# A hybrid mLSTM, window attention and expert layer on one core: narrow loads, gate columns, output-gate weights and row maxima rearranged in the input and mLSTM stages

## The reference, cut to what matters

```python
h = _rmsnorm(x, norm_mix); z = h @ w_in
gates = mif + b_if
ig, logf = gates[..., :4], log_sigmoid(gates[..., 4:])
# _mlstm, one step per chunk of 128 tokens, four heads of width 256
bcum = cumsum(fc)
dlog = where(causal, bcum[:, None] - bcum[None, :] + ic[None, :], -inf)
mt = maximum(bcum + m, max(dlog, -1))             # the row maximum
dmat = exp(dlog - mt[:, None]); sc = exp(bcum + m - mt)
s = (q @ k.T) * dmat
num = s @ v + sc * (q @ c);  den = sum(s) + sc * (q @ n)
hout = num / maximum(abs(den), exp(-mt))
c_new = wc * c + kw.T @ v;   n_new = wc * n + sum(kw)
```

## Time and profile before

| what | value |
|---|---|
| times of three runs | 2022.81, 2023.15 (median), 2028.75 us |
| the profiled execution | 2026.17 us, its span 2024.5 us, mean granted TensorE clock 0.943 |
| busy: PE, PEld, DVE, ACT, POOL | 88%, 83%, 42%, 34%, 17% of the span |
| the four heads, by PE's time line | about 51 to 628 us |
| DMA | 280.67 MB, 139 GB/s over the span |

### The profile page before, as it was taken

How to read it: one execution, slowest core, us unless ns; L and a number is a source line. 1 busy time by engine, 2 the same in 40 slices (tenths; PEclk the granted TensorE clock), 3 DMA queues, 4 the chain that set the end, 5 groups by cost and what they waited for, 6 DMA issues and landing times.

```text
span 2024.5 us, 33235 instructions
## 1 busy us (share of the span) xinstructions
PE 1787.5 (88%) x12631; PEld 1682.0 (83%) x12632; DVE 857.2 (42%) x1589; ACT 697.3 (34%) x1221; POOL 344.1 (17%) x275
## 2 busy tenths in 40 slices
PE   5989998998999999999999958989899469999960
PEld 4978997988989999899999948979899369998850
DVE  5423123122122110444444444233522659998856
ACT  4323122222222221332233333121202348888742
POOL 3001001001001000000000022000002037776634
PEclk9989999999999999999999978989999779999985
DMA  5033205105115222232222134332413369999967
GB/s 173 1 105 106 92 22 164 54 8 169 42 34 176 88 81 88 73 109 68 68 68 69 55 144 149 123 100 86 161 54 133 124 224 371 380 373 367 364 222 261
DMA packets 142962, 280.67 MB, mean 139 GB/s; under 512 B 35844, under 2 KB 106252, under 8 KB 130540
## 3 DMA queue, kind: packets, MB, share of 16 engines
q1 hardware_dynamic: 104608, 210.57, 30.3%
q0 software_dynamic: 18768, 48.79, 6.7%
q10 hardware_dynamic: 19488, 19.87, 2.8%
HBM read 227.36 MB, written 69.70 MB: 147 GB/s over the span
## 4 chain that ended last, share of the span: by engine, by line
PE 78%; DMA 8%; DVE 5%; issue 4%; ACT 2%; SPq 1%; POOL 1%; DVEq 0%; POOLq 0%; ACTq 0%; PEldq 0%
PE pb L770 18%; PE pb L771 17%; PE pb L772 17%; DMA stg<-in_w_gate_e 5%; PE pw L1057 3%; PE pq L1077 3%; PE pb L1065 2%; PE pw L770 2%; PE pw L771 2%; PE pw L772 2%; PE pw L861 1%; PE pq L844 1%; ACT aTh L1274 1%; PE pq L770 1%; PE pq L854 1%
## 5 line engine op out<-in xcount | busy, mean ns | idle before, releaser
L770 PE MATMUL pb<-aTh,wlo 128*128 128x352 f32 x1152 | 388.0, 337 | 29.3 <-issue 16.0
L770 PE MATMUL pb<-whi,aTl 128*128 128x256 f32 (+1 forms) x1296 | 377.3, 291 | 8.5 <-DVE aTl L2053 3.8
L771 PE MATMUL pb<-aTl,whi 128*128 128x352 f32 x1152 | 379.0, 329 | 0.0
L772 PE MATMUL pb<-aTh,whi 128*128 128x352 f32 x1152 | 378.9, 329 | 0.0
L771 PE MATMUL pb<-wlo,aTh 128*128 128x256 f32 (+1 forms) x1296 | 367.6, 284 | 0.0
L772 PE MATMUL pb<-whi,aTh 128*128 128x256 f32 (+1 forms) x1296 | 365.5, 282 | 0.0
L770 PEld LDWEIGHTS pb<-aTh,wlo 128*128 128x128 f32 x1152 | 225.0, 195 | 33.8 <-issue 27.1
L770 PEld LDWEIGHTS pb<-whi,aTl 128*128 128x128 f32 (+1 forms) x1296 | 234.8, 181 | 21.6 <-issue 11.8
L1644 DVE TENSOR_TENSOR wlo<-stage,whi 128x2048 fp32r<-128x2048 f32 x74 | 169.2, 2288 | 182.8 <-ACT whi L1274 182.8
L772 PEld LDWEIGHTS pb<-whi,aTh 128*128 128x128 f32 (+1 forms) x1296 | 235.7, 182 | 0.9
L771 PEld LDWEIGHTS pb<-wlo,aTh 128*128 128x128 f32 (+1 forms) x1296 | 234.4, 181 | 2.1
(11 more groups left out here) (396 smaller groups left out, 3020.4 us busy)
## 6 DMA issues: line engine op xcount, KB each, us to landing
stg<-in_w_down_e SPq DMA_DIRECT2D x32, 1024.0 KB, 14.1
stage<-in_w_in SPq DMA_DIRECT2D x30, 1024.0 KB, 5.3
stage<-in_w_gate_e SPq DMA_DIRECT2D x16, 1024.0 KB, 13.8
stage<-in_w_up_e SPq DMA_DIRECT2D x16, 1024.0 KB, 14.8
stg<-in_w_gate_e SPq DMA_DIRECT2D x16, 1024.0 KB, 14.7
stg<-in_w_up_e SPq DMA_DIRECT2D x16, 1024.0 KB, 15.0
zt_scratch<-zo ACTq DMA_DIRECT2D x80, 128.0 KB, 1.7
zg_scratch<-go ACTq DMA_DIRECT2D x48, 176.0 KB, 1.8
```

Source lines behind the costliest of these rows:

```text
L770: pe.matmul(out, ll, rh, start=first, stop=False)
L771: pe.matmul(out, lh, rl, start=False, stop=False)
L772: return pe.matmul(out, lh, rh, start=False, stop=last)
```

## The change

1. **Input loads.** `cst` is issued ahead of `gB`. The second, third and fourth x tiles follow the first without a narrow load between; `wif` is loaded after the fourth, `bif` after the last. The splits of `wif` move from step 2 to step 5 (ACT) and from step 4 to step 7 (DVE).
2. **Gate columns.** PE transposes them between feature groups 10 and 11 of the first head, not after group 11: four tiles into each of the two banks, the ninth and the state rows into `pw`, without waiting for a copy. DVE copies four tiles at once.
3. **Loads of a head.** `weights(3)` is issued before the wait for the gate columns and the state loads.
4. **Row maxima.** `nmrow` is split once into three bf16 terms, at partitions 0, 32 and 64 of `nmt`. Each head copies a selecting column (ones in the head's three rows) into `hrow`; the product in `s1` and in `head_sets` is now `hrow` by `nmt` in bf16 with K=68. The multiplication into `nmh` is gone.

```diff
@@ -34,2 +34,3 @@
 MH, MD = 4, 256
+NM = 64 + MH
 AH, AG, AD = 16, 4, 64
@@ -140,3 +141,4 @@
             msampb = a1("msampb", [TS, TS], BF16)
-            ones4 = a1("ones4", [MH, 128])
+            hsel = a1("hsel", [NM, MH])
+            hrow = a1("hrow", [NM, 128], BF16)
             gcol = a1("gcol", [128, NT, 128])
@@ -144,4 +146,3 @@
             wcb = a1("wcb", [128, 2 * NB])
-            nmrow = a1("nmrow", [MH, T + 2 * NB])
-            nmh = a1("nmh", [MH, T + 2 * NB])
+            nmt = a1("nmt", [NM, T + 2 * NB], BF16)
             Ce = a1("Ce", [128, 2, MD + 1])
@@ -170,2 +171,4 @@
             with sg:
+                nmrow = alloc(sg, "nmrow", [MH, T + 2 * NB])
+                nmb = alloc(sg, "nmb", [MH, T + 2 * NB], BF16)
                 gi = alloc(sg, "gi", [MH, T])
@@ -578,5 +583,5 @@
                 if t == 0:
-                    sp.dma_start(gB[:, :], norm_mix.to_broadcast([128, D])).then_inc(ld_c, 16)
                     sp.dma_start(cst[:, :], cst_d).then_inc(ld_c, 16)
-                if t == 1:
+                    sp.dma_start(gB[:, :], norm_mix.to_broadcast([128, D])).then_inc(ld_c, 16)
+                if t == NX - 1:
                     sp.wait_ge(init_v, 1)
@@ -585,5 +590,5 @@
                         sp.dma_start(wif[:, :, 32:36], wi[:, :, C_IF + 4:C_IF + 8]).then_inc(ld_g, 16)
-                        for g in range(2):
-                            sp.dma_start(bif[:, g:g + 1], b_if[:, g * MH:(g + 1) * MH].rearrange(
-                                "o h -> h o")).then_inc(ld_g, 16)
+            with nc.allow_non_contiguous_dma(reason="eight values"):
+                for g in range(2):
+                    sp.dma_start(bif[:, g:g + 1], b_if[:, g * MH:(g + 1) * MH].rearrange("o h -> h o")).then_inc(ld_b2, 16)
             sp.dma_start(nrow[0:2 * MH * NB, :], state_n[0].rearrange("b h (c p) -> (b h c) p", p=128)
@@ -594,3 +599,4 @@
                 weights(2, cols(wi, h * CW + C_MV), h, 4)
-                sp.wait_ge(gq_c, NT)
+                weights(3, cols(wi, h * CW + C_AQ), h, 4)
+                sp.wait_ge(gq_c, 3)
                 sp.wait_ge(st_s, h * (NB * 16) + 16)
@@ -599,3 +605,2 @@
                         "o (c p) e -> p (o c) e", p=128)).then_inc(ld_s, 16)
-                weights(3, cols(wi, h * CW + C_AQ), h, 4)
             for j in range(2):
@@ -828,3 +833,3 @@
                     pe.matmul(b[0:n, 0:n], kT[:, d, tok(c)], qT[:, d, tok(c)], start=(d == 0), stop=(d == 1))
-                pe.matmul(b[0:n, 128:128 + n], ones4[:, 0:n], nmh[:, tok(c)], start=True, stop=False)
+                pe.matmul(b[0:n, 128:128 + n], hrow[:, 0:n], nmt[:, tok(c)], start=True, stop=False)
                 mk = mcausb if c < NT - 1 else msampb
@@ -890,10 +895,10 @@
                 pe.wait_ge(gv_r, 1)
-                for t in range(NT):
-                    if t >= 2:
-                        pe.wait_ge(gq_c, t - 1)
-                    pe.transpose(AB[t % 2][:, 0:128], gq[:, t * 128:(t + 1) * 128], ident).then_inc(gq_t, 1)
+                for t in range(NPT):
+                    mm = pe.transpose(AB[t // 4][:, t % 4 * 128:(t % 4 + 1) * 128], gq[:, tok(t)], ident)
+                    if t % 4 == 3:
+                        mm.then_inc(gq_t, 1)
                 pe.wait_ge(n_rows, 16)
-                pe.transpose(pw[:, 0, 0:2 * MH * NB], nrow[0:2 * MH * NB, :], ident[0:2 * MH * NB, 0:2 * MH * NB]
-                             ).then_inc(gq_t, 1)
-                pe.wait_ge(gq_c, NT)
+                pe.transpose(pw[:, 0, 0:128], gq[:, TP:TP + 128], ident)
+                pe.transpose(pw[:, 0, 128:128 + 2 * MH * NB], nrow[0:2 * MH * NB, :],
+                             ident[0:2 * MH * NB, 0:2 * MH * NB]).then_inc(gq_t, 1)
 
@@ -902,3 +907,3 @@
                 pe.wait_ge(m_t1, M(h, -1))
-                pe.matmul(pq[:, 1, 0:2 * NB], ones4[:, :], nmh[:, T:T + 2 * NB], start=True, stop=True
+                pe.matmul(pq[:, 1, 0:2 * NB], hrow[:, :], nmt[:, T:T + 2 * NB], start=True, stop=True
                           ).then_inc(h_wc, 1)
@@ -923,6 +928,7 @@
                         used(G_M + j, h, 30)
-                with pe.If(h < 1):
-                    gate_columns()
-                with pe.Else():
-                    pe.nop()
+                    if j == 10:
+                        with pe.If(h < 1):
+                            gate_columns()
+                        with pe.Else():
+                            pe.nop()
                 head_sets(h)
@@ -1302,4 +1308,4 @@
                     i_.then_inc(x_hi, 1)
-                if t == 2:
-                    act.wait_ge(ld_g, 64)
+                if t == 5:
+                    act.wait_ge(ld_g, 32)
                     copy(wifh[:, :, :], wif[:, :, :]).then_inc(gw_h, 1)
@@ -1307,2 +1313,3 @@
 
+            act.wait_ge(ld_b2, 32)
             for g in range(NG):
@@ -1658,2 +1665,5 @@
             ve.tensor_copy(msampb[:, :], C("msamp", TS))
+            ve.tensor_tensor(hsel[:, :], C("ident", NM)[:, 0:MH], C("ident", NM)[:, 32:32 + MH], ALU.add)
+            ve.drain()
+            ve.tensor_tensor(hsel[:, :], hsel[:, :], C("ident", NM)[:, 64:64 + MH], ALU.add)
 
@@ -1684,3 +1694,3 @@
                     i_.then_inc(x_lo, 1)
-                if t == 4:
+                if t == 7:
                     ve.wait_ge(gw_h, 1)
@@ -1748,7 +1758,20 @@
                 ve.nop().then_inc(gv_r, 1)
-                for t in range(NT):
-                    ve.wait_ge(gq_t, t + 1)
-                    ve.tensor_copy(gcol[:, t, :], AB[t % 2][:, 0:128]).then_inc(gq_c, 1)
-                ve.wait_ge(gq_t, NT + 1)
-                ve.tensor_copy(ncol[:, :, :, :].rearrange("p b h c -> p (b h c)"), pw[:, 0, 0:2 * MH * NB])
+                ve.tensor_copy(nmt[0:MH, :], nmrow[:, :])
+                ve.drain()
+                ve.tensor_tensor(nmrow[:, :], nmrow[:, :], nmt[0:MH, :], ALU.subtract)
+                ve.drain()
+                ve.tensor_copy(nmb[:, :], nmrow[:, :])
+                ve.drain()
+                ve.tensor_tensor(nmrow[:, :], nmrow[:, :], nmb[:, :], ALU.subtract)
+                ve.tensor_copy(nmt[32:32 + MH, :], nmb[:, :])
+                ve.drain()
+                ve.tensor_copy(nmt[64:64 + MH, :], nmrow[:, :])
+                for g in range(2):
+                    ve.wait_ge(gq_t, g + 1)
+                    ve.tensor_copy(gcol[:, 4 * g:4 * g + 4, :], AB[g][:, :].rearrange("p (t c) -> p t c", t=4)
+                                   ).then_inc(gq_c, 1)
+                ve.wait_ge(gq_t, 3)
+                ve.tensor_copy(gcol[:, NT - 1, :], pw[:, 0, 0:128])
+                ve.tensor_copy(ncol[:, :, :, :].rearrange("p b h c -> p (b h c)"), pw[:, 0, 128:128 + 2 * MH * NB]
+                               ).then_inc(gq_c, 1)
                 ve.drain()
@@ -1762,4 +1785,3 @@
                 ve.wait_ge(st_pc, h * 16 + 16)
-                ve.tensor_scalar(nmh[:, :], nmrow[:, :], cst[0:MH, bass.ds(h + OFF["ident"][0], 1)], None,
-                                 ALU.mult)
+                ve.tensor_copy(hrow[:, :], hsel[:, bass.ds(h, 1)].to_broadcast([NM, 128]))
                 for q in range(4):
```

More of the change, by code:

```diff
@@ L183, in build @@
                 kwb = alloc(sc_, "kwb", [128, 2, MD])
+                alloc(sc_, "padc", [128, 1668])
                 zo = [alloc(sc_, f"zo{i}", [128, CW]) for i in range(2)]
@@ L337, in build @@
         ld_g = sem("ld_g")
+        ld_b2 = sem("ld_bif")
         ld_k = sem("ld_k")
@@ L578, in _ @@
                 if t == 0:
+                    sp.dma_start(cst[:, :], cst_d).then_inc(ld_c, 16)
                     sp.dma_start(gB[:, :], norm_mix.to_broadcast([128, D])).then_inc(ld_c, 16)
-                    sp.dma_start(cst[:, :], cst_d).then_inc(ld_c, 16)
-                if t == 1:
+                if t == NX - 1:
                     sp.wait_ge(init_v, 1)
@@ L1649, in _ @@
             ve.memset(mhalf[:, :], -0.5).then_inc(init_v, 1)
-            ve.memset(ones4[:, :], 1.0)
+            ve.memset(nmt[:, :], 0.0)
             ve.memset(v1[:, :, MD:MD + 1], 1.0)
@@ L1695, in gates @@
                 ve.wait_ge(z_ev, NG)
-                ve.wait_ge(ld_g, 64)
+                ve.wait_ge(ld_b2, 32)
                 ve.wait_ge(ld_k, 32)
@@ L1871, in _ @@
                 head_end(h)
-            ve.wait_ge(gq_t, NT + 2)
+            ve.wait_ge(gq_t, 4)
             ve.tensor_copy(nrow[:, :], pq[0:2 * MH * (NB + 1), 0, 0:128]).then_inc(gq_c, 1)
@@ L2386, in _ @@
                 gp.dma_start(hm_d[TP:T, bass.ds(h * MD, MD)], nd[0:TS, NPT, 0:MD]).then_inc(st_hm, 16)
-            gp.wait_ge(gq_c, NT + 1)
+            gp.wait_ge(gq_c, 4)
             gp.dma_start(s_n[0].rearrange("b h (c p) -> (b h c) p", p=128), nrow[0:2 * MH * NB, :]).then_inc(st_m, 16)
```

## The result

The changed kernel takes 1992.47 us (median of 4 runs, 1989.55 to 1994.62) against 2023.56 (4 runs, 2022.81 to 2028.75): a ratio of 0.9835, interval 0.9815 to 0.9855. The forecast was 1993. The profiled execution took 1994.4 us and has a span of 1992.7 us (2024.5 before).

A forecast was written before the change was run, and what follows sets the result against it. PE was taken to bound the kernel, with 78% of the chain that ends last. Terms 7.6+5.3+12.6+0.9+4 = 30.4 off the profiled 2026.17 gave 1995.8; that execution lying 3.0 above the median, 1993 us was forecast, range 1979 to 2007.

The forecast's parts named there:

- Bound: PE holds 78% of the chain that ends last; time taken off its row in the heads comes off the end.
- A: Input x tiles at the start: earlier loads make no difference, 0; bounds 2.1 us gained or 1 lost.
- B: Gate columns, first head: PE's wait at `head_sets` and the low clock behind it go, 7.6 us; bounds 5 to 8.
- C: Output-gate weights, first head: PE's 2.21 us wait and 3.10 of slowed work go, 5.3 us; bounds 3.5 to 5.5.
- D: Row maxima: the bf16 product saves 0.35 us in 36 chunks, 12.6, plus 0.9 in `head_sets` of three heads.
- both at 0.12: Upper case for the row maxima's chunks: both bf16 products, row and mask, cost 0.12 us, gaining 16.
- Small products stay dear: Rival: D gives only 5.8 us and F nothing, 19.6 in all, so 2003.5 us; chance 0.18.
- E: First-head test moved between feature groups 10 and 11: 0; hidden there it gives back 1.0 us in all.
- Slower: Rival: the branch between groups 10 and 11 costs PE 8.1 us in each of four heads, so 2029; chance 0.03.
- F: PE's three loop returns: state loads issued later shorten the 16.0 us of stalls by a quarter, 4; bounds nothing to 23.
- Returns of the loop go altogether: Rival: the stalls at the loop's returns vanish, 19 us more than F, so 1974; chance 0.07.

The follow-up runs named there:

- the second pair: The kernel before and the changed kernel each traced once more, nothing altered; the heads end at 625.87 and 594.97 us, 30.9 apart.
- p1_input: The kernel before with only the reordered input loads and row squares: 2025.92 us beside 2026.33, first gate product at 36.71, heads' end at 627.57.
- part 4 alone: The kernel before with only the row maxima as three bf16 terms, K=68: 13.7 us off 2028.15.
- part 2 alone: The kernel before with only the gate columns transposed before feature group 11: 9.4 us off 2028.15.
- unroll: The changed kernel with PE's loop over four heads written out, no first-head test: 1975.13 us, ratio 0.9748 to the kernel before.
- f32_k68: The changed kernel with the row maxima's product in float32 on 68 partitions, rows beyond the maxima zero: heads end at 600.37 us, tile 5.98.

## Why the prediction was right, step by step

- **Bound.** Right: time off PE's row in the heads came off the end, 31.8 of 35.0 in the traces (19.3 of 30.9 in the second pair, where the attention stretch alone differs by 9.7).
- **A**, 0: 0.4 in the changed kernel, within its bounds (0.8 alone in `p1_input`). The last `msq` was at 30.09 and not "near 31": the splits of `wif` did not eat the whole of the earlier arrival.
- **B**, 7.6: 7.6. L828, behind the first v group, started at 109.61 us, and L833, the same product after, at 101.62, 8.0 earlier, less A: 6.1 until the v group starts, 1.9 in the group itself, which takes 2.94 instead of 4.79. PE decided at `head_sets`, as argued, but at 98.47, 0.4 sooner.
- **C**, 5.3: 5.3. L849 moved by 11.3 us, but the tile behind it by 14.2 (125.46 to 111.25). Less the 8.0 and the 0.9 of D in two chunks that leaves 5.3. The wait was 2.21 here, but 1.2 in the second trace of the kernel before, so this exact meeting holds for one pair of traces. (The sum behind the 5.3 took 117.33 from the time line and 125.46 from the chain of waits, which puts the same product 0.16 later; with one view it is 5.15.)
- **D**, 12.6 and 0.9: the mechanism right, the first part too small, and the largest error. A chunk saved 0.45, so up to 36 x 0.45 = 16.2, the "both at 0.12" bound; part 4 alone took 15.9 off the heads. Pricing the product like the mask behind float32 (0.16) was wrong because that mask's 0.16 was itself dear by the 4 partitions ahead of it. The rival "Small products stay dear" fell: period 5.81. The prediction also says that this trace disagrees with what the Trainium skill ("TensorE: Matmul & The Clock Gate", section on LDWEIGHTS) says of weight loads; it had only the product's time for that, and the loads themselves agree (0.09 and 0.10 above). In `head_sets` the product gave 0.15 a head, 0.45 in three, not 0.9.
- **E**, 0: 0.9, at its bound of 1.0. In the chain of waits of the second head, from the last feature matmul to L903 pass 0.66 us before (252.63 to 253.29), and to L908 0.37 after (234.58 to 234.95); the product behind takes 0.39 and then 0.24 until the v group. The first shrinks with part 2 alone and not with part 4 alone, so it belongs to the moved test: 0.29 a head. The test was hidden in the stream between groups 10 and 11, at no cost that the trace shows, and the "Slower" rival fell.
- **F**, 4: 3.3 in the stalls; the clock behind them is not separated here. The quarter was a choice and came near, which is luck; that the loads and the stall coincide, which the term rests on, is shown. "Returns of the loop go altogether" needed the jump itself gone, as `unroll` shows. What that rival says of a body that just fits was not tested.

These make 0.4+7.6+5.3+16.2+0.45+0.9+3.3 = 34.2 of the 35.0 at the heads' end, where 30.4 were predicted; later stages took 3.2 back. That 1993 was met so closely is in part luck: a term too small by 3.6 and a later stage that lost time, one against the other. The second pair of traces, with 30.9 at the heads' end, would have met the 30.4 there and missed the end of the span by 11.

## What to carry to other kernels

A matmul over very few partitions is priced with the instruction behind it: padding the contraction with zero rows can be free and faster (`f32_k68`: 0.57 became 0.28 us with zeros alone). Of waits that stand one behind the other, removing one lengthens the next, so look at the next before adding gains up. When a change ends as large as forecast at its own stage and smaller at the end, compare the granted clock of unchanged stages, before seeking a new wait.

## What was not expected of the hardware

- The weights of a product on 4 partitions, and those of the product behind it, start to load only with their own product, where those around a product on 68 partitions start 0.06 to 0.11 us ahead: 0.10 us for each step into or out of such a product, which fits float32 and bf16.
- A stretch of the same work with eight waits of 1.7 us took between 333 and 343 us, by how often the granted clock was low behind a wait.
- A jump back over a body of some 1,900 PE records cost 4.0 to 4.4 us, with one packet of the instruction queue in it, and 5.1 to 5.6 when 2 MB of states were being loaded.
